# Gated linear attention in a two-layer trunk: level products two levels at a time, two heads per bank, and an exchange of value rows between partition halves

## What is computed

```
def step(state, inp):
    qi, ki, vi, bi = inp                      # bi: running sum of the log gates in the chunk
    o_inter = einsum('bhcd,bhde->bhce', qi * exp(bi), state)
    decay = exp(where(causal, bi[:, :, :, None, :] - bi[:, :, None, :, :], -inf))
    att = einsum('bhid,bhjd,bhijd->bhij', qi, ki, decay)
    o_intra = einsum('bhij,bhje->bhie', att, vi)
    b_last = bi[:, :, -1:, :]
    new_state = exp(b_last)[...] * state + einsum('bhjd,bhje->bhde', ki * exp(b_last - bi), vi)
    return new_state, o_inter + o_intra
```

## Time and profile before

| | us |
|---|---|
| runs shown, median (lowest, highest) | 502.76 (502.47, 502.80) |
| the profiled execution | 502.51 |
| its span, from the first to the last instruction | 500.8 |
| TensorE busy | 489.0 |
| GpSimd, VectorE, ScalarE busy | 335.8, 370.2, 253.0 |

### The profile page before, as it was taken

One profiled execution on the slowest core, in us unless ns is written; L12 is line 12 of the kernel. 1 busy time (PEld: TensorE's weight loads), 2 busy tenths in 40 slices (PEclk: granted clock), 3 DMA queues, 4 the chain that ended last, 5 costly groups with the idle time before them and its releaser, 6 DMA issues.

```text
span 500.8 us, 8321 instructions
## 1 busy us (share of the span) xinstructions
PE 489.0 (98%) x3135; PEld 395.4 (79%) x3135; DVE 370.2 (74%) x770; ACT 253.0 (51%) x416; POOL 335.8 (67%) x207
## 2 busy tenths in 40 slices
PE   7999999999999999999999999999999999999994
PEld 7977888777888788888888879887777778778883
DVE  3797599676996547466496373999999999758814
ACT  6735744331241433724476546657766656458203
POOL 5470759769984385566339947869999999940601
PEclk9999999999999999999999999999999999999999
DMA  8348243276548122202461532608877772411004
GB/s 278 105 150 281 85 133 121 69 272 227 170 187 282 62 85 84 86 1 84 149 274 31 137 84 86 168 23 190 191 189 179 181 195 83 165 70 57 0 1 168
DMA packets 50805, 67.41 MB, mean 135 GB/s; under 512 B 4648, under 2 KB 32339, under 8 KB 49742
## 3 DMA queue, kind: packets, MB, share of 16 engines
q1 hardware_dynamic: 50766, 66.89, 43.3%
HBM read 58.77 MB, written 7.91 MB: 133 GB/s over the span
## 4 chain that ended last, share of the span: by engine, by line
PE 90%; DVE 4%; POOL 3%; ACT 2%; issue 1%; POOLq 0%
PE bank L1866 35%; PE bank L1886 26%; PE bank L2204 7%; PE bank L2114 3%; PE bank L2091 3%; PE bank L2266 2%; PE bank L2253 2%; PE bank L2103 2%; PE bank L2028 1%; PE bank L1902 1%; PE bank L1797 1%; PE bank L2047 1%; POOL w_lo L678 1%; PE bank L1956 1%; PE bank L1807 1%
## 5 line engine op out<-in xcount | busy, mean ns | idle before, releaser
L678 POOL TENSOR_TENSOR w_lo<-w_raw,w_hi 128x2048 fp32r<-128x2048 f32 (+1 forms) x30 | 136.3, 4546 | 55.0 <-ACT w_hi L884 54.0
L1866 PE MATMUL bank<-hT_hi,w_hi 128*128 128x512 f32 (+1 forms) x280 | 110.5, 395 | 0.0
L1866 PE MATMUL bank<-hT_lo,w_hi 128*128 128x512 f32 (+1 forms) x280 | 110.4, 394 | 0.0
L1866 PE MATMUL bank<-hT_hi,w_lo 128*128 128x512 f32 (+1 forms) x280 | 109.7, 392 | 0.0
L1886 PE MATMUL bank<-w_hi,hT_hi 128*128 128x512 f32 x188 | 76.7, 408 | 0.0
L884 ACT ACTIVATE w_hi<-w_raw 128x2048 fp32r<-128x2048 f32 (+1 forms) x35 | 65.7, 1880 | 16.2 <-PE bank L1886 9.9
L1886 PE MATMUL bank<-w_hi,hT_lo 128*128 128x512 f32 x188 | 73.5, 391 | 0.0
L1886 PE MATMUL bank<-w_lo,hT_hi 128*128 128x512 f32 x188 | 73.3, 390 | 0.0
L1666 DVE SCALAR_TENSOR_TENSOR bank<-r_va,pvec,bank 128x512 f32<-128x512 f32 x94 | 69.1, 753 | 2.2
L1866 PEld LDWEIGHTS bank<-hT_lo,w_hi 128*128 128x128 f32 (+1 forms) x280 | 52.3, 187 | 15.4 <-issue 4.8
L1866 PEld LDWEIGHTS bank<-hT_hi,w_hi 128*128 128x128 f32 (+1 forms) x280 | 52.3, 187 | 12.9 <-issue 1.4
(11 more groups left out here) (285 smaller groups left out, 898.7 us busy)
## 6 DMA issues: line engine op xcount, KB each, us to landing
w_raw<-in_w_in_even_dram SPq DMA_DIRECT2D x14, 1024.0 KB, 5.4
w_raw<-in_w_in_odd_dram SPq DMA_DIRECT2D x16, 512.0 KB, 5.2
r_x<-in_w_out_even_dram SPq DMA_DIRECT2D x5, 1024.0 KB, 8.7
t_kept<-r_x SPq DMA_DIRECT2D x4, 1024.0 KB, 5.0
w_raw<-in_w_in_odd_dram SPq DMA_DIRECT2D x4, 1024.0 KB, 8.1
w_raw<-in_w_out_odd_dram SPq DMA_DIRECT2D x4, 1024.0 KB, 5.1
r_att<-u_kept SPq DMA_DIRECT2D x12, 258.0 KB, 4.5
r_ka<-u_kept SPq DMA_DIRECT2D x12, 258.0 KB, 4.5
```

Of the source, the lines that this page charges most:

```text
L678: nc.gpsimd.tensor_tensor(v(w_lo[j % 3]), v(raw(j)), v(w_hi[j % 3]).bitcast(F32), ALU.subtract).then_inc(lo_ready, 1)
L1866: ins = nc.tensor.matmul(proj_bank(g)[0:m, :], w[:, k, P * i:P * i + m], h[:, k, :], start=(n == 0), stop=(n == 3 * KC - 1))
```

## The change

- A level's scores of all four heads now fill two banks: bank r holds heads r and r + 2, so a fill is two heads and VectorE copies 8 blocks of 64 at a time. For odd heads chunk c goes to partition half (c + 1) % 2, the other one than before.
- So for odd heads the values must lie in the other half too: `vb_turned`, made by four transfers from SBUF to SBUF (64 partitions, 4 blocks of 512 bytes in each, 128 KB a transfer), issued by SP at j = 8 ahead of `load(8)`, behind a wait for the four copies of `vb`. The inside products of odd heads read it, and now go in the order of chunk and head.
- All seven key-value products are made in one insertion, two chunks to a bank; VectorE waits for the last before it starts the state updates.
- Levels go in as 0 and 32 after 18 matmuls of slot 7's second group, 16 and 8 after 4 matmuls of slot 9's first group, 4 and 2 after part 1 of slot 10, and 1 after part 5. VectorE's order of operands, copies and top-k halves is rewritten to match; the instructions are the same ones but for the copies.

```diff
@@ names and places
+        vb_turned = r_att[:, 1024:2048].rearrange("p (t i d) -> p t i d", t=TB, i=2)
...
-        level = lambda lv: [(lv, h) for h in range(BH)]
+        level = lambda lv: [(lv, r) for r in range(2)]
...
-        FILL_IN = {(7, 0): [("k0", "k1"), KV_FILLS[0:4], KV_FILLS[4:]], (7, 1): level(0), (8, 0): level(32), (8, 1): level(16),
-                   (9, 0): level(8), (9, 1): level(4)}
-        LEVEL_AFTER = {(10, 3): 2, (10, 7): 1}
+        LEVELS_IN = {(7, 1): (18, (0, 32)), (9, 0): (4, (16, 8))}
+        LEVELS_AFTER = {(10, 1): (4, 2), (10, 5): (1,)}
@@ SP, in the loop over j, ahead of load(j)
+                if j == 8:
+                    sp.wait_ge(act_emptied, evacs_through(FIRST[S_VB] + TB - 1, "act"))
+                    odd_heads = vb.rearrange("p t (i r d) -> p t i r d", i=2, r=2)[:, :, :, 1, :]
+                    for to, of in ((0, CH), (CH, 0)):
+                        for i in range(2):
+                            sp.dma_start(vb_turned[to:to + CH, :, i, :],
+                                         odd_heads[of:of + CH, :, i, :]).then_inc(vb_turned_in, 16)
                 if j == 10:
@@ VectorE, empty_fill
-                    lv, h = f
-                    a = attn[:, TB * h:TB * h + TB, :]
+                    lv, r = f
+                    a = attn[:, 2 * TB * r:2 * TB * r + 2 * TB, :]
                     dve.wait_ge(att_zero, 1)
+                    if lv:
+                        dve.wait_ge(fill_emptied, n - 1)
...
                 if f[:2] == "kv":
+                    dve.wait_ge(fill_done, FILL_NO[KV_FILLS[-1]] + 1)
+                    at = 256 * (t // 4)
@@ VectorE, the order
-            for f in level(0):
-                empty_fill(f)
+            empty_levels(0, 32)
             operand(16)
-            topk_half(2 * EARLY_ROUNDS + 1)
-            late = 2 * EARLY_ROUNDS + 2
-            for i, lv in enumerate(LEVELS):
-                for h in range(BH):
-                    empty_fill((lv, h))
-                topk_half(late + 2 * i)
-                if i + 2 < len(LEVELS):
-                    operand(LEVELS[i + 2])
-                topk_half(late + 2 * i + 1)
-            topk_half(late + 2 * len(LEVELS))
-            topk_half(late + 2 * len(LEVELS) + 1)
+            operand(8)
+            late_topk(1, 4)
+            empty_levels(16, 8)
+            late_topk(4, 5)
+            operand(4)
+            operand(2)
+            late_topk(5, 10)
+            empty_levels(4, 2)
+            late_topk(10, 11)
+            operand(1)
+            late_topk(11, 13)
+            empty_levels(1)
+            late_topk(13, 16)
@@ TensorE, chunk_products
-                    pe.wait_ge(fill_emptied, n + pair[-1] - 3)
...
-                            ins = nc.tensor.matmul(bank[4 + (n + e) % 4][p0:p0 + 64, DV * (h // 2):DV * (h // 2) + DV],
+                            ins = nc.tensor.matmul(bank[4 + (n + e) % 4][p0:p0 + 64, at:at + DV],
@@ TensorE, whole_level (was head_pair, called for heads 0 and 2)
+                for two in range(2):
+                    for c in range(NCHUNK):
+                        cols = slice(S * two + CH * c, S * two + CH * c + CH)
+                        for i in range(2):
+                            k0 = CH * ((c + i) % 2)
...
+                            at = n_q * (TB * two + c // 2)
+                            ins = nc.tensor.matmul(bank[4 + (n + i) % 4][k0:k0 + CH, at:at + n_q], keys, queries,
+                                                   start=True, stop=True)
@@ TensorE, outputs_b, inside
-                    for h in range(BH):
+                    pe.wait_ge(vb_turned_in, 16 * 4)
+                    for two in range(2):
                         for c in (2 * t, 2 * t + 1):
-                            k0 = CH * (c % 2)
-                            ins = add_to(h, c, attn[k0:k0 + CH, TB * h + t, :], vb[k0:k0 + CH, t, DV * h:DV * h + DV],
-                                         start=h < 2, stop=c == 0)
+                            for i in range(2):
+                                h, k0 = 2 * two + i, CH * ((c + i) % 2)
+                                v = vb_turned[k0:k0 + CH, t, two, :] if i else vb[k0:k0 + CH, t, DV * h:DV * h + DV]
+                                ins = add_to(h, c, attn[k0:k0 + CH, TB * (2 * i + two) + t, :], v,
+                                             start=two == 0, stop=c == 0)
@@ TensorE, among
+                if (s_, half) == (7, 0):
+                    return {6: lambda: key_rows(("k0", "k1")), 16: lambda: chunk_products(KV_FILLS)}
```

More of the change, by code:

```diff
@@ L437, in hybrid_trunk @@
         FILL_NO = {f: n for n, f in enumerate(FILLS)}
[L439 to L443 removed]
+        LEVELS_IN = {(7, 1): (18, (0, 32)), (9, 0): (4, (16, 8))}
+        LEVELS_AFTER = {(10, 1): (4, 2), (10, 5): (1,)}
+        LAST_FILL = {"k": FILL_NO["k1"], **{lv: FILL_NO[(lv, 1)] for lv in LEVELS}}
         NSTEP = TB * AH
@@ L1396, in empty_fill @@
                             out=chunk_state(t + 1)[:, DV * i:DV * i + DV], in0=chunk_state(t)[:, DV * i:DV * i + DV],
-                            scalar=chunk_decay[:, i, t:t + 1], in1=b[:, DV * i:DV * i + DV], op0=ALU.mult, op1=ALU.add)
+                            scalar=chunk_decay[:, i, t:t + 1], in1=b[:, at + DV * i:at + DV * i + DV], op0=ALU.mult, op1=ALU.add)
                     ins.then_inc(fill_emptied, 1)
@@ L1412, in _, with empty_levels, late_topk @@
             nc.vector.tensor_tensor(q_dec, q_dec, qbT, ALU.mult).then_inc(q_decayed, 1)
-            for f in level(0):
-                empty_fill(f)
-            operand(16)
-            topk_half(2 * EARLY_ROUNDS + 1)
-            late = 2 * EARLY_ROUNDS + 2
-            for i, lv in enumerate(LEVELS):
-                for h in range(BH):
-                    empty_fill((lv, h))
-                topk_half(late + 2 * i)
-                if i + 2 < len(LEVELS):
-                    operand(LEVELS[i + 2])
-                topk_half(late + 2 * i + 1)
-            topk_half(late + 2 * len(LEVELS))
-            topk_half(late + 2 * len(LEVELS) + 1)
+            def empty_levels(*lvs):
+                for lv in lvs:
+                    for f in level(lv):
+                        empty_fill(f)
+            def late_topk(first, last):
+                for i in range(first, last):
+                    topk_half(2 * EARLY_ROUNDS + i)
+            empty_levels(0, 32)
+            operand(16)
+            operand(8)
[11 more added lines that the diff above has]
+            late_topk(13, 16)
             topk_masks()
@@ L2007, in chunk_products, with whole_level @@
                                 ins.then_inc(fill_done, 1)
-            def head_pair(f):
-                lv, h = f
-                n = FILL_NO[f]
+            def whole_level(lv):
+                n = FILL_NO[(lv, 0)]
                 pe.wait_ge(fill_emptied, n - 2)
-                if h == 0 and lv:
+                if lv:
                     pe.wait_ge(operand_ready, ITEM_NO[lv] + 1)
-                at = S * (h // 2)
                 kk = lin[ITEM_NO[lv] % 4] if lv else kbT
                 qq = lin[ITEM_NO[lv] % 4] if lv else qbT
[L2019 to L2031, removed]
@@ L2033, in whole_level @@
-            def whole_level(lv):
-                head_pair((lv, 0))
-                head_pair((lv, 2))
+                for two in range(2):
[3 more added lines that the diff above has]
+                            k0 = CH * ((c + i) % 2)
+                            keys, queries, n_q = kk[64 * i:64 * i + 64, cols], qq[64 * i:64 * i + 64, cols], CH
+                            if lv:
+                                queries = queries.rearrange("p (a c) -> p a c", c=2 * lv)[:, :, lv:]
+                                n_q = CH // 2
+                            at = n_q * (TB * two + c // 2)
+                            ins = nc.tensor.matmul(bank[4 + (n + i) % 4][k0:k0 + CH, at:at + n_q], keys, queries,
+                                                   start=True, stop=True)
+                            if two and c == NCHUNK - 1:
+                                ins.then_inc(fill_done, 1)
@@ L2069, in outputs_b, with levels, among @@
                         ins.then_inc(fill_done, 1)
-            def among(fs):
-                if fs and fs[0] == ("k0", "k1"):
-                    jobs = [lambda: key_rows(fs[0])] + [(lambda f=f: chunk_products(f)) for f in fs[1:]]
-                else:
-                    jobs = [(lambda f=f: whole_level(f[0])) for f in fs if f[1] == 0]
-                return {(3 * KC * (i + 1)) // (len(jobs) + 1): job for i, job in enumerate(jobs)}
+            def levels(lvs):
+                for lv in lvs:
+                    whole_level(lv)
+            def among(s_, half):
+                if (s_, half) == (7, 0):
+                    return {6: lambda: key_rows(("k0", "k1")), 16: lambda: chunk_products(KV_FILLS)}
+                if (s_, half) in LEVELS_IN:
+                    n, lvs = LEVELS_IN[s_, half]
```

(7 more changed lines are left out.)

13 lines of the change are left out of this document (7 added, 6 removed).

## The result

The changed kernel takes 509.46 us, the median of four executions (509.07 to 511.31), against 502.74 for the kernel before on the same chip. The medians lie 6.7 us (1.3%) apart. The ratio on record, taken over all executions and not from the medians, is 1.0142 (95%: 1.0126 to 1.0157), so the change is slower by more than the noise. The forecast was 507.3 with a range of 504.0 to 512.0. The profiled execution took 509.07 with a span of 507.4 us, 6.56 us more than the one of before; forecast for it was +4.55.

The account below looks back on a forecast made before the run. TensorE, busy 98% of the span, was taken as the bound. The terms -0.3 - 1.5 - 1.65 + 5.4 + 2.6 = +4.55 on the profiled 502.51 gave 507.1, as a median 507.3 us, range 504.0 to 512.0.

Parts of the forecast that it names:

- main step: Late load(8) stops ScalarE some 7 us, so TensorE idles over 5 us ahead of the key-value products.
- Fewer insertions and outputs: On TensorE: key-value products' present wait gone -0.3, four fewer insertion switches -1.5, four-tile outputs with earlier copies -1.65.
- the 0.37 of the forecast: At each insertion on TensorE: the price of going into small tiles and out again, 0.37 us.
- rival 4: At the outputs: the tiles don't run four wide, +1.65, 508.9 us; chance 0.04.
- The exchange ahead of load(8): In SP's order: load(8) issued at 85.1, ScalarE stops 7.0 us, TensorE stands +5.4 us ahead of key-value products.
- The wait for operand(1): Ahead of level 1: TensorE's second wait, operand(1) ready at 151.3, TensorE there at 148.7; +2.6 us (0 to 4).
- The clock: After the key-value gap: half rate costs at worst 2.7 us, absorbed by the operand(1) wait; net 0 to 1.
- A gap of 5.4 us may just reach that: Ahead of the key-value products: TensorE's idle gap may just drop the granted clock from 2.4 to 1.2 GHz.
- Rival 1: At slot 8's split: the load's delay is hidden, the change gives what it removes; 500.3 us, chance 0.14.
- Rival 2: Only the wait ahead of the key-value products; operand(1) is in time at level 1; 504.7 us, chance 0.08.
- Rival 5: At load(8): it lands in well under 5.3 us, half of each wait goes; within 1 us of before, chance 0.04.
- Rival 3: On VectorE: operand(2)'s last multiply waits out GpSimd's slot 11 split, operand(1) 4.6 us later; 511.9 us, chance 0.08.

Follow-up runs that it names:

- e8: e1 with level 1 put after part 7 of slot 10 and VectorE's operand(1) brought ahead of three top-k halves; 499.32 us, ratio 0.9938.
- e7: e1 with one level per insertion, at the old places and in VectorE's old order; 500.57 us, ratio 0.9966.
- e1: The changed kernel with the exchange and its wait issued behind load(9) instead of ahead of load(8); 501.99 us, ratio 0.9991.
- e2: The kernel before plus the exchange's wait and four transfers ahead of load(8), and TensorE's wait for them at the outputs; 510.78 us, ratio 1.0166.
- e3: The kernel before plus only the wait for the last value row ahead of load(8), without transfers; 508.3 us, ratio 1.0113.
- e4: The changed kernel with 90 tiny bf16 matmuls on an unused bank ahead of the key-value products; 509.49 us, ratio 1.0141.
- e10: e9 with the 90 tiny bf16 matmuls ahead of the key-value products; 505.44 us, ratio 1.0056.
- e9: e8 with the exchange back ahead of load(8), as in the change; 507.86 us, ratio 1.0105.

## Why the prediction was right, and where it was not

The forecast (slower, inside the range, 2.2 us short) held at its main step and went wrong in one: its reason for counting the clock as nothing. That it came so near has some luck in it, since two misses offset each other: the second wait was 1.0 us shorter than forecast, and the clock took 2.2 at its place where the sum had nothing.

*Fewer insertions and outputs, forecast -0.3 - 1.5 - 1.65 = -3.45.* e8 gives -3.2. An insertion of two levels takes 2.00 us against twice 1.07 and less one way in and out; the 0.4 of e7 is the 0.37 of the forecast. The outputs' four tiles work as forecast. The first inside products in the timeline of the kernel after:

```profile
168.11 0.27 PE L2065 MATMUL bank<-r_vb,r_att 64*64 64x128 f32 x1
...
168.13 0.27 PE L2065 MATMUL bank<-r_att 64*64 64x128 f32 x1
168.22 0.27 PE L2065 MATMUL bank<-r_vb,r_att 64*64 64x128 f32 x1
```

Records of four products start within 0.02 us of each other, two with `vb`, two with `vb_turned`, and the next four 0.11 later: 0.027 each, the number taken from the key-value products. By the rule of the Trainium skill, TensorEngine Tiling (Array Packing), Gotcha 1: PSUM Pressure, the row groups that share a bank would have gone one after the other. They don't here, where the two write different partition halves of it, and rival 4 falls with it. But from the first record to the next full matmul the outputs take 172.59 - 167.91 = 4.68 us, not 4.3. The first batch and its copies save nearly what they should: 2.47 us in the timeline from its first record to that of the second (167.84 to 170.31), against 3.14 before, so 0.67 of the 0.75. The second batch takes 2.28 instead of 2.0. Timeline of TensorE in its middle:

```profile
170.71 0.27 PE L2065 MATMUL bank<-r_att 64*64 64x128 f32 x1
170.97 0.29 PE L2065 MATMUL bank<-r_vb,r_att 64*64 64x128 f32 x1
```

Timeline of VectorE, the copies out of the first batch:

```profile
169.45 1.42 DVE L1414 COPY r_ob<-bank 128x256 f32<-128x256 f32 x4 [4.95 <-PE bank L2065]
```

After 16 of the 32 inside records TensorE pauses: the next one starts 0.26 us later, when the fourth copy is out (169.45 + 1.42 = 170.87). The code makes this second block wait for the last two copies (`fill_emptied`). Before, 16 records took 16 x 0.055 = 0.9 us, longer than two copies. The forecast gave this second wait for copies nothing: the term was 0.4 too large, 0.3 of it here.

*The exchange ahead of load(8), forecast +5.4.* Load out at 85.1 (measured 85.36), landed at 90.4 (90.83), ScalarE stops for 7.0 (7.29), key rows done at 102.8 (103.1), TensorE stands for 5.4 (5.75). All of it is right to within 0.5 us, and e1, e2 and e3 show it by taking the cause away and by adding it alone.

*The wait for operand(1), forecast +2.6.* It is there, with its releaser as named, but 1.6 us long. TensorE came later than forecast, since the clock had cost it 2.2 us. VectorE came later too: operand(1) was ready at 152.82, not at 151.3.

*The clock, forecast 0 to 1.* This is the step that failed. It granted up to 2.7 us of loss at the place itself, which fits the 2.2 measured, but said that the wait for operand(1) absorbs it, for "that time doesn't hang on TensorE". But it does. Ahead of operand(4) in VectorE's order stand the copies of levels 16 and 8, and these wait for TensorE. The timeline of VectorE in the change:

```profile
129.91 0.78 DVE L1393 COPY_PREDICATED r_att<-level_mask,bank 128x256 f32<-128x256 uint8 x2 [3.89 <-PE bank L2051]
...
132.91 1.59 DVE L1368 TENSOR_TENSOR r_g<-r_g,r_qkb 128x512 f32<-128x512 f32 x1
```

TensorE makes those levels at 128.80, behind the products that ran at 1.2 GHz. So operand(4) starts at 132.91, where the forecast had 131.6, and doesn't wait for ScalarE any more. In e4, with the clock kept, the same multiply starts at 131.36, released by ScalarE's exponential as forecast, and level 1 starts at 151.63, where the forecast had 151.3. The chain of the forecast was thus right for a full clock. In the change TensorE came to level 1 at 151.4 instead of 148.7, and the operand was ready 1.5 later too. Of the 2.0 us that the forecast of the profiled execution lacks (6.56 against 4.55), 1.6 are there when level 1 starts (152.95 against 151.3): 1.3 by the clock, as e4 shows it, and 0.3 in pieces of VectorE's chain (the four multiplies beside `weight_sum` took 6.6, not 6.4). The other 0.4 is the outputs. So the wait absorbed 0.7 of the 2.2 (it is 2.28 in e4 and 1.56 in the change), and not nearly all. What was left of the clock's price, 1.3 at level 1, is 1.0 at the end of the two profiled executions and nothing between the medians (509.46 and 509.49). So the traces show that the reason was wrong; that the price lay above "0 to 1" isn't shown. "A gap of 5.4 us may just reach that" was careful in the wrong direction, too: e3's gap of 3.8 us was enough.

*The rivals.* Rival 1 described e1: no wait ahead of the key-value products, one of 1.5 at level 1, forecast 500.3, measured 500.74 in the profile, 501.99 in the median. Rival 2 (operand(1) in time, 504.7) is e10 if the clock is kept, at 505.44, and e9 if it falls, at 507.86. Rival 5, a load that lands in well under 5.3 us, falls with the 5.47 measured. Rival 3, a multiply caught by GpSimd's split of slot 11, didn't happen in any profile of a kernel with double insertions. It did in e7, which has VectorE's old order: there the multiply at 133.38 took 5.09 us beside a split that began at 132.84, as before the change, and TensorE didn't wait for it. Timeline of VectorE in the change (operand(2)'s last multiply, operand(1)'s last):

```profile
137.82 1.77 DVE L1369 TENSOR_TENSOR r_g<-r_g,r_qkb 128x512 f32<-128x512 f32 x1
...
151.05 1.75 DVE L1369 TENSOR_TENSOR r_g<-r_g,r_qkb 128x512 f32<-128x512 f32 x1
```

Timeline of GpSimd in the change:

```profile
132.64 6.41 POOL L732 TENSOR_TENSOR r_x<-r_x 128x512 f32<-128x512 f32 x4
139.01 5.06 POOL L687 TENSOR_TENSOR w_lo<-w_raw,w_hi 128x2048 fp32r<-128x2048 f32 x1
```

The split begins 0.6 us ahead of the last multiply's end. The multiply had begun 1.2 us before it and kept its 1.77 us; the split took 5.06, where the earlier trace rows has 4.57. The distance that the forecast put at 1.3 us was gone, yet the multiply, already under way, wasn't caught. Whether an execution of the change at 511.31, or one of e1 at 504.01, had a multiply caught there, stays open: the size would fit (a caught multiply took 5.05 instead of 1.8, 3.3 more), and both kernels lose most of their spread with the wait that would pass it on; but none was profiled.

## What to carry to other kernels

A wait put into a queue that works in order costs whatever stands behind it, not what it guards: here a wait for data that nobody needed for 75 us held back a prefetch and cost 5.6 us by itself (e3), 8.1 with the four issues behind it (e2). Moving it away was the larger part of the repair: e1 is level with the kernel before, and only with operand(1) in time as well do the 3.2 us of gain appear (e8). Put such a step behind the last prefetch whose consumer is near, and follow each engine's order one instruction further than the wait. When a wait leaves TensorE idle for some microseconds, add what the clock takes afterwards, unless the next wait on the way is for something that hangs on no TensorE result at all; that has to be read in the other engine's order too.

## What the runs showed of the hardware that was not expected

- The granted clock fell to 0.5 in gaps shorter than the 6.6 us of the earlier trace rows: in e3 TensorE waited 3.8 us ahead of the key-value products, whose first 32 records then took 1.98 us instead of 1.10. In the profile of e7 it fell at about 12.5 us, with no wait of TensorE over 0.7 us in the 9 us ahead of it; in e9, with waits of 0.7 and 0.5 in the same place, it stayed at 1.00. The low stretch also reached into the work behind the gap: in the change to almost 108 us, where the work had begun again at 103.14. Its price at the place depended on how much of it lay over the work: 2.2 us in the change, 1.5 in e9. 90 tiny matmuls in the gap held the clock at 1.00 in both windows of e4.
- VectorE and GpSimd stretch each other for longer than the earlier trace rows showed: a multiply of 128 x 512 takes 0.69 us alone (in the change's chain at 100.60), four in a row beside GpSimd's adds took 1.6 to 1.8 each, and the four adds 6.41 instead of 5.97.
